# Two-layer decoder trunk in float32: GLA's gate projections placed between the steps of its recurrence, the last output columns by token halves, and conv's first tap steps placed anew

## What is computed

```python
def reference(x, mem, ...):
    for i in range(2):
        x = layer_norm(ALPHA * x + 0.5 * swiglu(x, ffn1_w_gu[i], ffn1_w_down[i]), ...)
        if i % 2 == 0:
            y, qm = gla_mix(x @ gla_w_in[j], ...)
            w_out = gla_w_out[j]
        else:
            y, qm = conv_mix(x @ conv_w_in[j], ...)
            w_out = conv_w_out[j]
        m = mem_attention(qm, mem, mem_w_kv[i])
        x = layer_norm(ALPHA * x + jnp.concatenate([y, m], axis=-1) @ w_out, ...)
        x = layer_norm(ALPHA * x + 0.5 * swiglu(x, ffn2_w_gu[i], ffn2_w_down[i]), ...)
    return x

# gla_mix: q, k (512 columns each), v, r (1024 each), a (16), qm (512)
#   chunks of 64 tokens, 4 heads; state 128x256 per head
#   att = where(causal, qe @ ke.T, 0);  o = att @ v + qe @ state
#   state = state * exp(b_last) + kd.T @ v
#   o = o * rsqrt(mean(o^2) + eps) * g_onorm;  y = o * silu(r)
# conv_mix: a, gt, qm;  u = a * sigmoid(gt); depthwise conv, 31 taps; layer norm; silu
```

## Time and profile before

| | |
|---|---|
| median of 3 runs | 2168.29 us (2164.15 to 2170.86) |
| the profiled execution | 2170.72 us |
| its span in the profile | 2169.0 us |
| granted clock of PE, mean | 0.986 |
| busy | PE 2107.4 us, DVE 961.1, ACT 703.3, POOL 237.5 |

### The profile page before, as it was taken

How to read it: one execution, slowest core, us unless ns; L and a number is a source line. 1 busy time by engine, 2 the same in 40 slices (tenths; PEclk the granted TensorE clock), 3 DMA queues, 4 the chain that set the end, 5 groups by cost and what they waited for, 6 DMA issues and landing times.

```text
span 2169.0 us, 26384 instructions
## 1 busy us (share of the span) xinstructions
PE 2107.4 (97%) x10597; PEld 1782.8 (82%) x10597; DVE 961.1 (44%) x1298; ACT 703.3 (32%) x950; POOL 237.5 (11%) x170
## 2 busy tenths in 40 slices
PE   8999999999989999999999999999999899999998
PEld 7888887977778888888799888879887688888887
DVE  3333323433434553333344333335699763333335
ACT  5322222264513243332225333223342433222223
POOL 4221000053303220000002000001100221000000
PEclk9999999999989999999999999999999899999999
DMA  6644222332201324433232444222543122222232
GB/s 217 215 136 154 97 83 90 99 108 78 78 1 59 97 88 135 155 135 112 81 128 88 155 135 155 83 99 101 194 136 151 58 97 97 97 97 87 80 98 65
DMA packets 208429, 239.65 MB, mean 110 GB/s; under 512 B 4656, under 2 KB 200366, under 8 KB 206301
## 3 DMA queue, kind: packets, MB, share of 16 engines
q1 hardware_dynamic: 207740, 236.40, 32.7%
q10 hardware_dynamic: 608, 2.13, 0.2%
HBM read 216.49 MB, written 22.02 MB: 110 GB/s over the span
## 4 chain that ended last, share of the span: by engine, by line
PE 83%; DVE 7%; ACT 4%; issue 3%; DMA 1%; POOL 1%; DVEq 0%; POOLq 0%; ACTq 0%; SPq 0%
PE bank L1363 23%; PE bank L1365 23%; PE bank L1364 23%; DVE u L1301 3%; PE bank L1370 2%; PE bank L1371 2%; PE bank L1372 2%; PE bank L1441 1%; ACT whi L517 1%; ACT u L611 1%; PE bank L1800 1%; DVE u L1095 1%; PE bank L1446 1%; DVE wlo L909 1%; POOL wlo L419 1%
## 5 line engine op out<-in xcount | busy, mean ns | idle before, releaser
L517 ACT CAST whi<-raw 128x2048 fp32r<-128x2048 f32 (+2 forms) x198 | 334.8, 1691 | 1099.2 <-PE bank L1365 1014.2
L1363 PE MATMUL bank<-xhi,whi 128*128 128x512 f32 x1632 | 638.5, 391 | 6.6 <-DVE bk L1173 3.3
L1365 PE MATMUL bank<-xhi,wlo 128*128 128x512 f32 x1632 | 635.7, 390 | 0.0
L1364 PE MATMUL bank<-xlo,whi 128*128 128x512 f32 x1632 | 635.6, 389 | 0.0
L909 DVE TENSOR_TENSOR wlo<-raw,whi 128x2048 fp32r<-128x2048 f32 (+2 forms) x167 | 339.7, 2034 | 586.7 <-ACT whi L517 575.9
L1363 PEld LDWEIGHTS bank<-xhi,whi 128*128 128x128 f32 x1632 | 306.7, 188 | 71.7 <-DVE bk L1173 3.7
L1365 PEld LDWEIGHTS bank<-xhi,wlo 128*128 128x128 f32 x1632 | 306.7, 188 | 64.3
L1364 PEld LDWEIGHTS bank<-xlo,whi 128*128 128x128 f32 x1632 | 306.8, 188 | 63.3 <-issue 0.2
L1363 PE MATMUL bank<-h_hi,whi 128*128 128x512 f32 x528 | 208.0, 394 | 3.3 <-DVE wlo L909 3.3
L1365 PE MATMUL bank<-h_hi,wlo 128*128 128x512 f32 x528 | 205.5, 389 | 0.0
L1364 PE MATMUL bank<-h_lo,whi 128*128 128x512 f32 x528 | 205.5, 389 | 0.0
(11 more groups left out here) (281 smaller groups left out, 2664.9 us busy)
## 6 DMA issues: line engine op xcount, KB each, us to landing
raw<-in_ffn_w_gu_dram SPq DMA_DIRECT2D x88, 1024.0 KB, 4.9
raw<-in_ffn_w_down_dram SPq DMA_DIRECT2D x32, 896.0 KB, 4.6
raw<-in_ffn_w_down_dram SPq DMA_DIRECT2D x32, 512.0 KB, 3.4
raw<-in_gla_w_in_dram SPq DMA_DIRECT2D x13, 1024.0 KB, 5.1
raw<-in_conv_w_in_dram SPq DMA_DIRECT2D x10, 1024.0 KB, 6.3
early_raw<-in_conv_w_in_dram SPq DMA_DIRECT2D x18, 512.0 KB, 5.3
lo_scratch<-early_lo SPq DMA_DIRECT2D x18, 512.0 KB, 4.1
raw<-in_mem_w_kv_dram SPq DMA_DIRECT2D x8, 1024.0 KB, 6.2
```

The costliest lines, as they stand in the source:

```text
L517: nc.scalar.copy(whi[:, s, 0:kc, 0:width], raw[:, s, 0:kc, 0:width]).then_inc(hi_ready, 1)
L1363: nc.tensor.matmul(to, whi[:, s, k, w], hi, start=start, stop=False)
L1364: nc.tensor.matmul(to, whi[:, s, k, w], lo, start=False, stop=False)
L1365: return nc.tensor.matmul(to, wlo[:, s, k, w], hi, start=False, stop=stop)
```

## The change

It has four parts. (a) v is computed with tokens as rows at once (`values`), by 96 matmuls of 128x256 per chunk, and the transposes and their copies go. (b) The 192 matmuls of r are cut into 32 units of six (`gates_of_r`) and placed between the steps of the recurrence, around outputs(0,3) of the memory attention, and around the RMS norm's sums and broadcasts; O uses two banks in place of four. The 16 diagonal blocks of the RMS norm become four operations, and POOL's split of chunk 15 moves ahead of its power. (c) In both output projections the last two pairs of blocks (512 columns), not one, are computed by token halves, with their A weights in a spare buffer (`a_spare`) that ACT and POOL fill early. The order of PE there is half 0 pairs 0 and 1, half 1 pair 0, half 1 pair 1. (d) The low part of conv's chunk 2 is made by DVE from `raw` and not loaded; the glu and maxima steps between the taps move by one or two steps.

The diff, cut to its core:

```diff
-HALVED = [6, 6, 6, 6, DK, 6, 6]
+HALVED = [6, 4, 6, 6, DK, 4, 6]
...
-OUT_BANKS = [(0, 1), (2, 3), (0, 1), ((2, 3), (4, 6))]
+OUT_BANKS = [(0, 1), (2, 3), ((0, 1, 2, 3), (0, 1, 2, 3))]
...
-            for j in range(2, 10):
+            load(n + 4, 0, cols(w, CONV_COLS[4]))
+            for j in range(3, 10):
...
+            def spare_lo_parts(ln, n0):
+
+                to = a_spare(ln)
+                for i in range(2):
+                    pool.wait_ge(hi_ready, n0 + 4 + i + 1)
+                    pool.wait_ge(lo_ready, n0 + 4 + i)
+                    nc.gpsimd.tensor_tensor(to[:, 1, A_K * i:A_K * i + A_K, :], raw[:, i, 0:A_K, :],
+                                            to[:, 0, A_K * i:A_K * i + A_K, :].bitcast(F32), ALU.subtract).then_inc(lo_ready, 1)
...
+            split_lo(GLA_N + 15, 1)
             pool.wait_ge(rms_var, 1)
             nc.gpsimd.tensor_tensor(rms_r, rms_v, minus_half, ALU.pow).then_inc(rms_rs, 1)
-            split_lo(GLA_N + 15, 1)
-            with pool.Fori(0, 2) as q:
-                split_lo(GLA_OUT_N + 4 * q, 0, A_K)
...
+            split_lo(GLA_OUT_N, 0, A_K)
+            split_lo(GLA_OUT_N + 1, 1, A_K)
+            split_lo(GLA_OUT_N + 3, 1, B_K, after_dve=True)
+            spare_lo_parts(LN_GLA_OUT, GLA_OUT_N)
+            split_lo(GLA_OUT_N + 7, 1, B_K, after_dve=True)
...
+                for i in range(2):
+                    act.wait_ge(raw_loaded[i], 16 * (t0 + 3 if n0 < DIAG_N else t0 + 1))
+                    nc.scalar.copy(a_spare(ln)[:, 0, A_K * i:A_K * i + A_K, :], raw[:, i, 0:A_K, :]).then_inc(hi_ready, 1)
...
+                split_hi(t0 + 3, 0, B_K, used=n0 + 3)
...
+            def r_evac(j):
+                act.wait_ge(w_used, GLA_N + 12 + j + 1)
+                for t in range(2):
+                    nc.scalar.activation(r_act(2 * j + t), bank[R_BANK[j][t]][:, :], ACT.Silu).then_inc(gla_evac, 1)
...
             for h in range(HEADS):
                 if h + 1 < HEADS:
                     kd_evac(h + 1)
+                if h % 2 == 0:
+                    r_evac(h // 2)
                 for e, tmp in ((0, exp_a), (1, exp_b)):
-                    b = bank[2 * (h % 2) + e][:, :]
+                    b = bank[e][:, :]
                     act.wait_ge(o_mm, 2 * h + e + 1)
                     nc.scalar.copy(u[:, 2 * h + e, :], b).then_inc(o_read, 1)
...
+                if h % 2 == 0:
+                    step(12 + h // 2)
+            for k in range(8):
+                if k in (0, 2):
+                    step(14 + k // 2, A_K)
+                    r_evac(2 + k // 2)
+                if k == 6:
+                    split_hi(GLA_OUT_N // 2 + 1, 0, B_K)
...
+                for h in range(2):
+                    for d in (4, 6):
+                        if h == 0:
+                            scaled_x(ln, d)
+                            scaled_x(ln, d + 1)
+                        half_block(ln, h, d, n0 + 8, 1.0, OUT_BANKS[2])
+                        half_block(ln, h, d + 1, n0 + 8, 1.0, OUT_BANKS[2])
+                        half_square(ln, h, d)
+                        half_square(ln, h, d + 1)
+                        if h and d == 4:
+                            split_lo(n0 + 8, 0)
+                    if h:
+                        split_lo(n0 + 9, 1)
+                    norm(ln, h)
...
-                diagonals(ke[:, h, :], rms_r[:, TB * h:TB * h + TB], rms_diag)
+                nc.vector.tensor_tensor(
+                    ke[:, h, :].rearrange("p (b c) -> p b c", b=TB),
+                    ident[:, :].rearrange("p (a c) -> p a c", a=1).to_broadcast([P, TB, P]),
+                    rms_r[:, TB * h:TB * h + TB].rearrange("p (b a) -> p b a", a=1).to_broadcast([P, TB, P]),
+                    ALU.mult).then_inc(rms_diag, 1)
...
-            split_lo(GLA_OUT_N + 2, 0)
+                if h == 2:
+                    split_lo(GLA_OUT_N + 2, 0)
...
+            split_lo(CONV_N + 2, 0)
             glu(0, 4)
-            taps(0, {14: [(glu, 1, 8)], 29: [(maxima, 1, 0)]})
+            taps(0, {15: [(glu, 1, 8)], 30: [(maxima, 1, 0)]})
             dve.wait_ge(taps_done, 2 * WIDTH)
             dve.sem_inc(y_evac, 1)
-            taps(1, {2: [(normalise, 1, 0)], 15: [(maxima, 1, 1), (glu, 2, 16), (mo_lo_part, 1, 0)],
-                     18: [(cin_lo_parts,), (after_diagonals,), (normalise, 1, 1)]})
+            taps(1, {2: [(normalise, 1, 0)], 17: [(maxima, 1, 1), (glu, 2, 16), (mo_lo_part, 1, 0)],
+                     20: [(cin_lo_parts,), (after_diagonals,), (normalise, 1, 1)]})
...
+                if HALVED[ln] == 4:
+                    pe.wait_ge(y_half, half_no(ln, 1, 5) + 1)
                 for h in range(2):
...
+            def out_halves(ln, n0, mo_hi, mo_lo, y_h, y_l):
...
+                    for p in range(2):
+                        pe.wait_ge(lo_ready, n0 + 7 + p)
+                        if h == 0:
+                            pe.wait_ge(y_evac, Y_BASE[ln] + 2 * p + 2)
+                        else:
+                            pe.wait_ge(y_half, half_no(ln, 0, 5 + 2 * p) + 1)
+                        for t in range(2):
+                            to = bank[OUT_BANKS[2][h][2 * p + t]]
+                            for k in range(A_K):
+                                mm3_half(h, to, spare[:, 0, A_K * p:A_K * p + A_K], spare[:, 1, A_K * p:A_K * p + A_K], k, t,
+                                         mo_hi, mo_lo, k, h == 0 and k == 0, False)
+                            for k in range(B_K):
+                                last = mm3_half(h, to, whi[:, p], wlo[:, p], k, t, y_h, y_l, k, False, k == B_K - 1)
+                            if h == 0 or t == 0:
+                                last.then_inc(y_even, 1)
+                            else:
+                                last.then_inc(w_used, 1 if p else 3)
+                            if h == 1 and p == 0:
+                                if t == 0:
+                                    sums(ln, 0)
+                                else:
+                                    spread_rstd(ln, 0)
...
-                chunk(n0 + 4 + j, j % 2, (2 * (j % 2), 2 * (j % 2) + 1))
+                if j < 4:
+                    chunk(n0 + 4 + j, j % 2, (2 * (j % 2), 2 * (j % 2) + 1))
+                else:
+                    values(j)
+
+            def values(j):
+
+                pe.wait_ge(lo_ready, n0 + 4 + j + 1)
+                for b in range(TB):
+                    to = bank[2 * (j % 2) + b // 2][:, (b % 2) * 256:(b % 2) * 256 + 256]
+                    tok = slice(b * P, (b + 1) * P)
+                    for k in range(DK):
+                        nc.tensor.matmul(to, xhi[:, k, tok], whi[:, j % 2, k, :], start=(k == 0), stop=False, skip_group_check=True)
+                        nc.tensor.matmul(to, xhi[:, k, tok], wlo[:, j % 2, k, :], start=False, stop=False, skip_group_check=True)
+                        last = nc.tensor.matmul(to, xlo[:, k, tok], whi[:, j % 2, k, :], start=False, stop=(k == DK - 1),
+                                                skip_group_check=True)
+                last.then_inc(w_used, 1)
...
+            def gates_of_r(first, count):
+
+                for i in range(first, first + count):
+                    j, k = divmod(i, DK)
+                    if k == 0:
+                        pe.wait_ge(lo_ready, n0 + 12 + j + 1)
+                        if j < 3:
+                            pe.wait_ge(gla_evac, 21 + 2 * j)
+                        else:
+                            pe.wait_ge(o_read, 16)
+                    for t in range(2):
+                        last = mm3(bank[R_BANK[j][t]][:, :], j % 2, k, t, xhi[:, k, :], xlo[:, k, :], k == 0, k == DK - 1)
+                    if k == DK - 1:
+                        last.then_inc(w_used, 1)
...
-            pe.wait_ge(v_evac, 8)
             keys_and_att(0)
+            gates_of_r(0, 2)
+            outputs(0, 3)
+            gates_of_r(2, 2)
+            pe.wait_ge(mo_done, 4)
             for h in range(HEADS):
                 pe.wait_ge(kdt_evac, h + 1)
                 state_sums(h, range(4))
                 if h + 1 < HEADS:
                     keys_and_att(h + 1)
+                gates_of_r(4 + 4 * h, 2)
                 state_sums(h, range(4, 7))
+                gates_of_r(6 + 4 * h, 2)
                 pe.wait_ge(att_evac, h + 1)
                 for e in range(2):
-                    to = bank[2 * (h % 2) + e]
-                    if h >= 2:
-                        pe.wait_ge(o_read, 4 * (h - 2) + 2 * e + 2)
+                    to = bank[e]
+                    if h:
+                        pe.wait_ge(o_read, 4 * (h - 1) + 2 * e + 2)
...
+            gates_of_r(20, 4)
+            for h in range(HEADS):
+                pe.wait_ge(ss_done, h + 1)
+                for b in range(TB):
+                    last = nc.tensor.matmul(bank[4][:, TB * h + b:TB * h + b + 1], ke[:, h, b * P:(b + 1) * P],
```

(10 more changed lines are left out.)

174 lines of the change are left out of this document (63 added, 111 removed).

## The result

The changed kernel takes 2143.03 us (median of 4 runs, 2141.05 to 2144.93), the kernel before 2166.22 us beside it: ratio 0.9895, interval 0.9878 to 0.9912, so about 1% faster, and clear of the 0.3% that the prediction took for the scatter. The forecast was 2136 with a range of 2128 to 2150, so the direction and the range held, and the size was 7 us too good. The profiled execution took 2144.93 us, 25.8 less than that of before, where 31.8 were forecast.

What follows compares the result with a forecast made beforehand. PE was taken as the bound, busy 2107.4 of 2169.0 us, so only its idle or low-clock stretches could be won. 2170.7 − 20.6 − 8.8 − 2.4 = 2138.9, less 2.4 to the median: 2136 predicted, range 2128 to 2150.

Steps and rivals of the forecast that it cites:

- the cost of the weights: Output projections: a new PE wait of 0.9 us, as the last B pair loads only after the spare copy, then splits.
- terms B and C: The two output projections, second out_b to end of ffn's first chunks: 78.8 us become 74.5, −4.4 each, −8.8 together.
- Term A: GLA from v's transposes to out_b: r fills waits at full clock, 124.3 to 101.2 us; with v's added cost, −20.6.
- silu wait: In GLA, PE waits 0.5 us for ACT's last silu of r ahead of out_a.
- A change from float32 to r's matmuls: In GLA, some 10 more changes between small float32 matmuls and r's, at 0.2 us each, cost 2.0 us.
- The diagonals' wait of 1.0: In GLA, PE waits 1.0 us (bounds 0 and 2.4) for the RMS norm's diagonals, DVE being held by POOL's split.
- Rival R1: The recurrence's O parts: the clock falls in spite of filled gaps, +10 to +13 us, 2147; chance 0.11.
- In every case with a low clock a gap of 1.4 us or more stood ahead: Argument from the earlier trace's recurrence against a low clock in the O parts once the gaps are filled.
- R2: Output projections' tails give nothing because weight loads come 2 to 3 us late: +8.8 us, 2145; chance 0.10.
- Term D: Conv's start: PE's 2.53 us wait for the load of wlo goes, as DVE makes the split; −2.4 us, bound 0.
- the glu one tap step later: Conv's taps: with this (0.7) and sigmoids 2.5 us earlier, 3.2 of DVE's 3.57 us wait goes, some 0.4 left.
- R3: Conv: PE keeps the gain at the start but loses it again at mo_lo; +2.4 us, 2139; chance 0.08.

Runs made afterwards that it cites:

- experiment 1: The changed kernel with one wait added: in conv's output projection POOL starts the spare splits only after DVE has written residual block 0; 2137.28 us, ratio 0.9858.
- experiment 7: The changed kernel with part (c) undone in both output projections and no spare weights; 2147.51 us, ratio 0.9914.
- experiment 8: On hold, glu, maxima and further steps between conv's taps put back to 14, 29, 15 and 18; 2138.78 us, ratio 0.9871.
- hold: The changed kernel with the one added wait of experiment 1; 2137.28 us, ratio 0.9858.
- the first kernel of experiment 6: On hold, the RMS norm's diagonals as before the change: 16 operations of 128x128 with one tensor input, for four of 128x512; 2136.97 us, ratio 0.9863.
- experiments 2 and 4: r moved at the RMS sums: changed kernel, 48 matmuls ahead 2146.83, one unit per head 2144.98; on hold, per head 2138.80, silu earlier 2139.16, one unit mid-sums 2139.63 us.

## Why the prediction held, and where it missed

**The step that failed is the cost of the weights in terms B and C.** It priced the spare splits by when PE needs them ("0.9 for the weights") and did not ask whom POOL's two new operations hold. In the paragraph ahead of it the prediction had read from the earlier trace rows that a POOL split holds DVE, and used it for the diagonals alone. In conv the splits follow POOL's c_lo at once and meet the residual of block 0, on which PE's shift sum waits: +4.2 us, and some 1.7 more by the low clock behind that wait. One wait on POOL takes it away (experiment 1), and so does undoing part (c) (experiment 7). The Trainium skill, page "SBUF — State Buffer", section "Who interferes with whom", names tensor_scalar too among the operations that can contend with GpSimd. The traces agree: 2.56 us in place of 0.43 for the one ahead of the residual, and 7.52 in place of 3.23 for the old form of the diagonals, which is not free of the hold either.

**Term A.** The mechanism was right in all parts: no waits for states, clock 1.00 through the recurrence, v chunks of 11.6 to 11.7 us (11.5 forecast), silu wait 0.44 (0.5). From keys_and_att(0) to out_b(0) it is 102.3 us at 0.97, where 101 were forecast. Two sizes were off. A change from float32 to r's matmuls costs 0.34 − 0.23 = 0.11 us, not 0.2 (600.66 to 601.00), so about 1 us was saved. And the clock's fall at the RMS sums cost 3.3 (4.0 for 3.5 and 8.2 for 5.4), which no term had. The diagonals' wait of 1.0 was covered by it; at full clock (experiment 1) it was 0.53. Without the fall A is −22.6 (696.01 for the shift sum in experiment 1).

**Rival R1** forecast a fall of the clock in the O parts. They ran at 1.00; another, smaller fall came, at the RMS sums, which the rival did not name. "In every case with a low clock a gap of 1.4 us or more stood ahead" holds for heads 1 to 3 of the trace of before (1.44, 1.80 and 2.92); right ahead of its first fall, 593 to 597, stood gaps of 1.06 and 0.68. And it is no rule: here the fall came with PE busy without a gap.

**Terms B and C** measured −5.1 and −3.6 against −4.4 each (78.8 less the 74.5 of the working is 4.3; 4.4 is a slip). The wait of 0.9 for the weights did not come. In both projections a POOL split of 4.62 us held one of DVE's additions for the norm (4.68 us, where the next of the kind took 0.69), and PE waited 0.8 us for DVE's residual behind it. What sets C apart from B is the low clock behind the wait of 5.33. R2 did not happen.

**Term D** measured −2.8 (forecast −2.4). Its first half was right: the load's wait goes, DVE's taps pace the end of the stage (52.4 us without a gap ahead of PE's wait for mo_lo), and DVE has to make up on the way what PE gains. It does, because ACT's sigmoids come earlier. The other half, that the glu one tap step later is needed for it, was not: with the old steps DVE still waits 0.90 of the 3.57 us, and that comes out of the slack of 2.5 us that it has with the new ones (experiment 8). R3 did not happen.

**From sum to median.** The profiled execution was 1.9 us above its median, 2.4 assumed. Of the 6.0 us between the 2138.9 of the sum and the profiled time, 4.2 are conv's new wait, 1.4 the last stores, 0.8 term A with the clock's fall in it (3.3, against savings that the sum did not have), and B, C and D together −0.3, though C holds some 1.7 of low clock; 0.1 is rounding.

The best ratio measured is that of hold, 0.9858 for 0.9895, at 2137.3 us; the first kernel of experiment 6 cannot be told from it (2137.0, 0.9863). That this lies within 1.3 us of the forecast is partly luck: errors of both signs cancel in the sum.

## What to carry to other kernels

Before you give POOL a new two-input operation, look at what DVE does in those microseconds, and not only at when its result is needed: the held one ended only 0.2 to 0.6 us behind POOL's operation, however short it is alone (0.43 and 0.69 us), and here one wait on POOL won some 4 us of waiting and the low clock behind it, for 1.1 us of a new wait. Fill PE's waits with matmuls of another product that need nothing from the engine waited for: 13.5 us here, where 9.3 us of waits came back without it and most of the rest was clock. Where PE and the chain behind a reduction are nearly level, what puts the reduction off is mostly paid back in waits, and a wait of 2 to 3 us can cost the clock as well (experiments 2 and 4).

## What was not expected of the hardware

- The clock fell with PE busy in every microsecond, at 32 float32 matmuls of one column (0.86 over their 4 us, 0.65 over the next 8.2), in five of six executions of the same code, and in none of four with six wide matmuls behind each eight of them.
- Behind a wait of 2.5 to 2.75 us for one and the same load the clock stayed at 1.00 in one kernel's execution and fell to 0.77 over 5 us in another's.
- A DVE operation with one tensor input and a scalar (128x512, 0.43 us) took 2.56 us beside a POOL split of 2.4, as one with two inputs did (0.69, then 2.71).
